# One-core decoder layer: branch and filler weights asked for two slots ahead, negations and DRAM additions of w_down spread over other stages

## The chip, the cores and the metric

One NeuronCore of a Trainium2 chip runs the whole kernel. The metric is the device time of one execution in microseconds. The engines are TensorE (PE, with its weight loads as PEld), VectorE (DVE), ScalarE (ACT), GpSimd (POOL) and SyncE (SP, which here only issues transfers). Each of them works through its own list in order and waits on semaphores.

## The reference

One decoder layer on x (512 tokens, 2048 features, float32), with weights in float32. Cut to what matters here:

```
h = rms_norm(x) ; (q, k, v ..., m_a, m_b) = split(h @ w_in)
y_nsa = nsa_attention(...)          # 8 heads
y_fox = fox_attention(...)          # 8 heads
merged = sigmoid(m_a) * (y_nsa @ w_branch_nsa) + sigmoid(m_b) * (y_fox @ w_branch_fox)
x = x + merged @ w_out
u, v = split(rms_norm(x) @ w_up) ; u = causal_dwconv(u)      # width 3, D_FF = 5632
x = x + (gelu(u) * v) @ w_down
return rms_norm(x)
```

## The kernel before

Products are made to full float32 accuracy from a high and a low part: for weights W, ACT makes `w_hi`, DVE makes `w_lo = w_raw - w_hi`, and PE forms hi·hi, hi·lo and lo·hi. The stages follow each other in time: the paired QKV products (to 580 us), compression of keys and values, NSA (8 heads), merge A (`w_branch_nsa`), FOX (8 heads), merge B (`w_branch_fox`), W_out, the up stage (44 units in a loop), the down stage. QKV, up and down use products of 2x2 blocks in the manner of Strassen; for the down stage sums and differences of blocks of w_down are needed, and they are made ahead of time in DRAM (tensors w_s1, w_s2, w_n3, w_n4, shown as `w_s` and `w_n`).

**Slots.** Outside QKV, up and down, weights come in slots of 1 MB. `w_raw`, `w_hi` and `w_lo` each have two buffers. SP's `load(s, src)` (L493 to L498) waits until `w_lo` of slot s-2 is made, and loads slot s. ACT's `hi(s)` (L1354) waits for the load and for PE to have used slot s-2. DVE's `lo(s)` (L1910) follows it. A merge has 8 slots of 48 matmuls each; slot p makes output blocks 2p and 2p+1.

**Merge.** SP's `load_merge` (L629 on) issues for each slot the weights and, with `load_gates` (L636), the gates of the next slot into one of two buffers `gate_t`. `load_gates(p)` waits until DVE has multiplied the outputs of slot p-2 (semaphore `br_read`). ACT then takes the sigmoid of the gates, and DVE multiplies (L2264; L2266 and L2267 in merge B). ACT's list is sigmoid(p), hi(p+1), sigmoid(p+1), ...; DVE's is lo(p+1), multiply(p), lo(p+2), ...

**Filler.** While a head of NSA or FOX waits for its softmax, PE works on one slot of plain gate blocks (`slot_cols`, L804 to L806). In FOX, SP loads slot S_FOX+2+h at the start of its iteration h (after the store of `o_fox`, L593); ACT makes `hi` of that slot in head h ahead of the head's exponentials (L1555), then POOL scales the probabilities (L2664), and PE transposes them (L1079).

**POOL's background work.** A negation loads a quarter (512 KB) of two w_down blocks into SBUF (L2677), negates it (L2683) and stores it (L2685): 40 of them. A DRAM addition has four steps (L2691 to L2699), with two, two, one and one transfers of 1 MB, of which four accumulate in DRAM: 10 times. Each step waits for the landing of the one before it. Before, negations 0 to 23 stand in QKV, 24 to 31 in merge A and 32 to 39 in merge B; additions 0 and 1 in NSA, 2 and 3 in merge A, 4 and 5 in FOX, 6 and 7 in merge B, 8 and 9 in W_out. In the up stage POOL only multiplies v by the GELU of u (L2746).

**Up stage.** SP loads w_up into `raw` (L697, L700) and stores the product of POOL (L705); a unit takes one turn of about 20 us.

**Start of compression.** SP reads `kv_fm` back (L587, two transfers), loads `sel` (L588), stores the last unit of QKV (L536, L538) and only then goes on. ACT and DVE wait for the landing of that store before `hi` and `lo` of slot S_PRE+1.

## Time and profile before

| | us |
|---|---|
| median of three runs | 2813.95 |
| the runs | 2813.82, 2817.32, 2813.95 |
| the profiled execution | 2819.67 |
| its span | 2817.7 |

The profiled execution is 5.7 us above the median. The stage windows below are in microseconds from the start of its span. PE is busy for 95% of the span, DVE 71%, ACT 43%, POOL 19%.

### The profile page before, as it was taken

How to read it: one execution, taken by the hardware profiler on the slowest of the kernel's cores; microseconds unless marked ns; L12 is line 12 of the kernel's file. 1: busy time of each engine (PE TensorE's matmuls, PEld its weight loads, DVE VectorE, ACT ScalarE, POOL GpSimd, SP SyncE). 2: the span in 40 equal slices, each digit the busy share in tenths (PEclk: the TensorE clock that was granted, in tenths of full speed). 3: DMA queues.
4: the chain of work that ended last, by engine and by line, in shares of the span. 5: the costliest groups of instructions: out<-in, count | busy, mean ns of one | idle time of the engine just before them, and what ended most of it. 6: DMA issues, size and time to landing. Idle time of an engine off the chain costs nothing.

```text
span 2817.7 us, 39923 instructions
## 1 busy us (share of the span) xinstructions
PE 2674.0 (95%) x14729; PEld 2300.1 (82%) x14729; DVE 2003.6 (71%) x2529; ACT 1225.1 (43%) x1614; POOL 539.4 (19%) x385
## 2 busy tenths in 40 slices
PE   8999999989996888778999999999999999999998
PEld 6899999978885676656888999999999998888886
DVE  5898888855551233224228999999999998888886
ACT  6444444434441133212235555555555554444445
POOL 0144444413433322332100000000000000000002
PEclk9999999999998999988999999999999999999999
DMA  7556666585558977689952544444343545666664
GB/s 226 149 174 195 180 189 184 159 244 153 139 136 235 253 174 199 180 236 268 242 183 83 135 116 118 124 111 129 105 131 104 134 107 188 235 224 224 224 209 150
DMA packets 499190, 489.52 MB, mean 174 GB/s; under 512 B 11566, under 2 KB 376832, under 8 KB 498310
## 3 DMA queue, kind: packets, MB, share of 16 engines
q1 hardware_dynamic: 457204, 371.37, 44.2%
q0 software_dynamic: 36080, 106.33, 15.6%
q10 hardware_dynamic: 5826, 10.76, 1.1%
q8 instruction: 50, 0.82, 0.1%
q14 instruction: 30, 0.25, 0.0%
HBM read 425.46 MB, written 127.96 MB: 196 GB/s over the span
## 4 chain that ended last, share of the span: by engine, by line
PE 81%; DMA 9%; DVE 3%; ACT 3%; issue 2%; SPq 1%; POOL 1%; DVEq 0%; ACTq 0%
PE bank L854 22%; PE bank L863 14%; PE bank L1336 13%; PE bank L856 11%; PE bank L804 6%; PE bank L806 6%; PE bank L805 6%; DMA w_raw<-in_w_branch_nsa_dram 3%; DMA w_raw<-in_w_branch_fox_dram 3%; DMA w_raw<-in_w_in_dram 2%; PE bank L1085 2%; ACT w_hi L1354 1%; PE bank L1079 1%; DVE w_lo L1910 1%; POOL l_fox L2664 1%
## 5 line engine op out<-in xcount | busy, mean ns | idle before, releaser
L1910 DVE TENSOR_TENSOR w_lo<-w_raw,w_hi 128x2048 fp32r<-128x2048 f32 x59 | 136.2, 2308 | 349.4 <-ACT w_hi L1354 349.4
L854 PE MATMUL bank<-hl,ring_hi 128*128 128x512 f32 x1032 | 368.4, 398 | 0.5 <-ACT v_sb L1722 0.5
L1336 PE MATMUL bank<-fold_hi,y_slot 128*128 128x512 f32 x1120 | 344.9, 389 | 0.0
L856 PE MATMUL bank<-hl,ring_lo 128*128 128x256 f32 x1032 | 289.8, 281 | 0.0
L1354 ACT ACTIVATE w_hi<-w_raw 128x2048 fp32r<-128x2048 f32 x59 | 112.9, 1913 | 356.4 <-DMA w_raw<-in_w_branch_fox_dram 107.5
L1336 PEld LDWEIGHTS bank<-fold_hi,y_slot 128*128 128x128 f32 x1120 | 210.3, 188 | 43.7
L2746 POOL TENSOR_TENSOR v_sb<-v_sb,conv_t 128x512 f32<-128x512 f32 x44 | 65.3, 1483 | 919.5 <-ACT conv_t L1736 906.1
L1818 ACT ACTIVATE fold_hi<-x_raw 128x1024 fp32r<-128x1024 f32 x140 | 148.5, 1063 | 201.8 <-PE bank L1336 199.7
L854 PEld LDWEIGHTS bank<-hl,ring_hi 128*128 128x128 f32 x1032 | 194.0, 188 | 46.9 <-ACT v_sb L1722 0.7
L1698 ACT ACTIVATE ring_hi<-s_a 128x1024 fp32r<-128x1024 f32 x129 | 136.9, 1062 | 202.7 <-PE bank L856 107.4
L854 PE MATMUL bank<-hl,q_ring_hi 128*128 128x512 f32 x600 | 215.8, 401 | 2.3 <-issue 1.8
L1336 PE MATMUL bank<-fold_lo,y_slot 128*128 128x512 f32 x560 | 217.8, 389 | 0.0
L856 PEld LDWEIGHTS bank<-hl,ring_lo 128*128 128x128 f32 x1032 | 195.1, 189 | 0.0
L2524 DVE TENSOR_TENSOR fold_lo<-x_raw,fold_hi 128x1024 fp32r<-128x1024 f32 x140 | 172.0, 1230 | 24.3 <-ACT fold_hi L1818 24.3
L804 PE MATMUL bank<-y_hi,w_hi 128*128 128x512 f32 x256 | 111.7, 436 | 80.6 <-DVE w_lo L1910 80.6
L804 PE MATMUL bank<-hl,w_hi 128*128 128x512 f32 x448 | 181.9, 406 | 4.4 <-DVE w_lo L1920 3.8
L806 PE MATMUL bank<-hl,w_lo 128*128 128x512 f32 x448 | 176.5, 394 | 0.0
L805 PE MATMUL bank<-hl,w_hi 128*128 128x512 f32 x448 | 176.0, 393 | 0.0
L856 PE MATMUL bank<-hl,q_ring_lo 128*128 128x256 f32 x600 | 169.2, 282 | 0.0
L2345 DVE TENSOR_TENSOR ring_lo<-raw,ring_hi 128x1024 fp32r<-128x1024 f32 x129 | 161.8, 1255 | 5.6 <-ACT ring_hi L1698 2.7
L2345 DVE TENSOR_TENSOR ring_lo<-s_a,ring_hi 128x1024 fp32r<-128x1024 f32 x129 | 157.5, 1221 | 6.0 <-ACT ring_hi L1698 5.9
L1416 ACT ACTIVATE q_ring_hi<-q_sum 128x1024 fp32r<-128x1024 f32 x75 | 79.6, 1061 | 161.5 <-DVE q_sum L2015 95.6
(388 smaller groups left out, 7137.5 us busy)
## 6 DMA issues: line engine op xcount, KB each, us to landing
raw<-in_w_up_dram SPq DMA_DIRECT2D x43, 1024.0 KB, 7.1
raw<-in_w_up_dram SPq DMA_DIRECT2D x86, 512.0 KB, 7.5
w_s<-in_w_down_dram POOLq DMA_DIRECT2D x30, 1024.0 KB, 13.1
x_raw<-in_w_down_dram SPq DMA_DIRECT2D x30, 1024.0 KB, 5.1
w_raw<-in_w_in_dram SPq DMA_DIRECT2D x26, 1024.0 KB, 7.7
raw<-in_w_in_dram SPq DMA_DIRECT2D x25, 1024.0 KB, 8.6
raw<-in_w_in_dram SPq DMA_DIRECT2D x50, 512.0 KB, 7.2
x_raw<-w_s SPq DMA_DIRECT2D x20, 1024.0 KB, 5.5
```

The lines of the kernel that those rows point to most:

```text
L804: mm(dst, l_hi, r_hi, start=first, stop=False)
L805: mm(dst, l_hi, r_lo, start=False, stop=False)
L806: return mm(dst, l_lo, r_hi, start=False, stop=final)
L854: mm(pb[bank][:], hi[:, w], high_low(y[0][:, k, :], y[1][:, k, :]), start=first and k == 0, stop=False, skip_group_check=True)
L856: last = mm(pb[bank][:, 0:TH], lo[:, w], y[0][:, k, :], start=False, stop=k == KH - 1, skip_group_check=True)
L863: last = mm(pb[bank][:, 0:TH], left[:, w], y[z][:, k, :], start=first and k == 0 and n == 0, stop=k == KH - 1 and n == 2, skip_group_check ...
L1336: last = mm(pb[banks[tt]][:], y[:, z, k, tk], right[:, w], start=first and k == 0 and m == 0, stop=k == 3 and m == 2, skip_group_check=True)
L1354: A(w_hi[:, s.par, :], w_raw[:, s.par, :], ACT.Copy).then_inc(w_hi_done, 1)
L1818: A(fold_hi[k % RING][:], x_raw[b][:, 1024 * h:1024 * h + 1024], ACT.Copy).then_inc(piece_hi, 1)
L1910: V.tensor_tensor(w_lo[:, s.par, :], w_raw[:, s.par, :], w_hi[:, s.par, :].bitcast(F32), ALU.subtract).then_inc(w_ready, 1)
L2345: V.tensor_tensor(ring_lo[b][:], src, ring_hi[b][:].bitcast(F32), ALU.subtract).then_inc(piece_ok, 1)
L2524: V.tensor_tensor(fold_lo[b][:], x_raw[FOLD_AT[p, n] % 4][:, 1024 * h:1024 * h + 1024], fold_hi[b][:].bitcast(F32), ALU.subtract).then_inc ...
```

## The change

1. `load_merge`: the weights of slot p+2 are now issued ahead of the gates of slot p+1; before, the weights of slot p+1 were issued behind the gates of slot p+1, whose issue waits for the multiplied outputs of slot p-1. The weights of slot 1 stand ahead of the stage's other waits. In merge A the last two turns load the first two slots of FOX.
2. FOX: iteration h loads slot S_FOX+3+h instead of S_FOX+2+h.
3. POOL: negations 24 to 28 in merge A (without additions), 29 to 34 one in each of the FOX heads 0 to 5 ahead of the addition step, 35 to 39 in merge B. Additions 2 and 3 in FOX, 4 and 5 after the negations of merge B, 6 to 9 in the up stage, one step after each of the multiplications of units 0 to 15. ACT waits for negation 34 before FOX head 6.
4. Compression: the `q_u` and `q_v` stores stand ahead of the second read of `kv_fm`; `sel` is loaded by POOL.
5. The semaphore `o_put` of the stores of plain blocks is split into two by parity; the waits ask for the same stores.

```diff
-QKV_QUARTERS, MERGE_QUARTERS = 24, 32
+QKV_QUARTERS, MERGE_QUARTERS = 24, 35
...
-        for part, (a, b) in enumerate(((0, 4), (4, 12))):
-            sp.dma_start(kv_fm[:, a:b, :], p_dram[kv_at + a:kv_at + b].rearrange("n p t -> p n t")).then_inc(kv_in[part], 16)
-        sp.dma_start(sel[:], c_sel).then_inc(kv_in[1], 16)
+        sp.dma_start(kv_fm[:, 0:4, :], p_dram[kv_at:kv_at + 4].rearrange("n p t -> p n t")).then_inc(kv_in[0], 16)
         store_qkv(QKV_UNITS - 1)
+        sp.dma_start(kv_fm[:, 4:12, :], p_dram[kv_at + 4:kv_at + 12].rearrange("n p t -> p n t")).then_inc(kv_in[1], 16)
...
+            def load_weights(p):
+                if p < 8:
                     load(slot(base + p), wbr[which][:, :, 256 * p:256 * p + 256], n=256)
+                elif which == 0:
+                    load_block(slot(base + p), PLAIN[p + 4])
+
+            load_weights(1)
...
+            load_gates(0)
+            load_weights(2)
+            load_gates(1)
+            store_plain((11, 21)[which], o_cover[:, 0, :])
+            for p in range(1, 8):
+                load_weights(p + 2)
...
                 if p < 7:
                     load_gates(p + 1)
...
+        load_block(slot(S_FOX + 2), PLAIN[14])
         for h in range(HEADS):
-            load_block(slot(S_FOX + 2 + h), PLAIN[14 + h])
+            if h < HEADS - 1:
+                load_block(slot(S_FOX + 3 + h), PLAIN[15 + h])
...
         pool.wait_ge(y_ok, 2)
-        quarters(6, 2)
+        negatives(QKV_QUARTERS, QKV_QUARTERS + 5)
         for h in range(HEADS):
             pool.wait_ge(fr_ready, h + 1)
             scale(l_fox, 4).then_inc(fp_ready, 1)
-            sums_in_dram(4 + h // 4, h % 4)
+            if h < HEADS - 2:
+                negatives(QKV_QUARTERS + 5 + h, QKV_QUARTERS + 6 + h)
+            sums_in_dram(2 + h // 4, h % 4)
         pool.wait_ge(y_ok, 4)
-        quarters(8, 6)
+        negatives(MERGE_QUARTERS, 4 * FOLD_UNITS)
         for k in range(8):
-            sums_in_dram(8 + k // 4, k % 4)
+            sums_in_dram(4 + k // 4, k % 4)
...
-        with pool.Fori(0, UNITS // 4) as i:
-            for r in range(4):
-                a_out_of(r, i)
+        for n in range(UNITS):
+            a_out_of(n % 4, n // 4)
+            if n < 16:
+                sums_in_dram(6 + n // 4, n % 4)
```

The instructions of PE, ACT and DVE keep their order; only SP and POOL are written in another order. At the start of merge A, SP's list before (L593 stores a block, L636 loads gates, L498 loads weights of a slot):

```order
181 L593 DMA p_dram<-o_nsa 128x512 x2
182 L636 DMA gate_t_93<-p_dram 128x2x512
183 L636 DMA gate_t_94<-p_dram 128x2x512
184 L593 DMA p_dram<-o_cover 128x512
185 L498 DMA w_raw<-in_w_branch_nsa_dram 128x8x256
186 L636 DMA gate_t_93<-p_dram 128x2x512
187 L498 DMA w_raw<-in_w_branch_nsa_dram 128x8x256
188 L636 DMA gate_t_94<-p_dram 128x2x512
```

And the same place now:

```order
180 L592 DMA p_dram<-o_nsa 128x512 x2
181 L498 DMA w_raw<-in_w_branch_nsa_dram 128x8x256
182 L635 DMA gate_t_93<-p_dram 128x2x512
183 L498 DMA w_raw<-in_w_branch_nsa_dram 128x8x256
184 L635 DMA gate_t_94<-p_dram 128x2x512
185 L592 DMA p_dram<-o_cover 128x512
186 L498 DMA w_raw<-in_w_branch_nsa_dram 128x8x256
187 L635 DMA gate_t_93<-p_dram 128x2x512
```

Two weight transfers (slots 1 and 2) have moved ahead of the second gates and of the `o_cover` store; from there on each weight transfer belongs to a slot one further on than before. Merge B has the same rows.

In FOX, POOL's list of one head before (`l_fox` is scaled, then an addition step):

```order
239 L2664 TENSOR_SCALAR l_fox<-l_fox,st 128x512
240 L2664 TENSOR_SCALAR l_fox<-l_fox,st 128x384
241 L2664 TENSOR_SCALAR l_fox<-l_fox,st 128x128
242 L2664 TENSOR_SCALAR l_fox<-l_fox,st 128x256
243 L2691 DMA w_n<-in_w_down_dram 512x512
244 L2692 DMA w_s<-in_w_down_dram 512x512
```

And now:

```order
219 L2675 TENSOR_SCALAR l_fox<-l_fox,st 128x512
220 L2675 TENSOR_SCALAR l_fox<-l_fox,st 128x384
221 L2675 TENSOR_SCALAR l_fox<-l_fox,st 128x128
222 L2675 TENSOR_SCALAR l_fox<-l_fox,st 128x256
223 L2688 DMA nb_late<-in_w_down_dram 128x2x512
224 L2694 TENSOR_SCALAR nb_late<-nb_late 128x1024
225 L2696 DMA w_n<-nb_late 128x2x512
226 L2702 DMA w_n<-in_w_down_dram 512x512
227 L2703 DMA w_s<-in_w_down_dram 512x512
```

A whole negation (load, negate, store) has come in between the scaling and the addition step of heads 0 to 5.

## Rows read from the trace of the kernel before

**Rows 1.** Shares of the chain that ended last, by line (the page)

```profile
PE bank L854 22%; PE bank L863 14%; PE bank L1336 13%; PE bank L856 11%; PE bank L804 6%; PE bank L806 6%; PE bank L805 6%; DMA w_raw<-in_w_branch_nsa_dram 3%; DMA w_raw<-in_w_branch_fox_dram 3%; DMA w_raw<-in_w_in_dram 2%; PE bank L1085 2%; ACT w_hi L1354 1%; PE bank L1079 1%; DVE w_lo L1910 1%; POOL l_fox L2664 1%
```

**Rows 2.** Busy time by stage: merge A, FOX, merge B, up; then PEclk, DMA share, GB/s

```profile
844.00:980.20 136.20, 100.23 (x385) 79.63 (x385) 27.75 (x23) 21.91 (x15) 50.06 (x33) 0.89 0.93 246
980.20:1157.00 176.80, 152.25 (x720) 120.25 (x719) 59.98 (x123) 62.69 (x122) 44.61 (x44) 0.94 0.71 178
1174.00:1316.60 142.60, 100.09 (x377) 79.25 (x378) 45.97 (x40) 27.31 (x18) 51.13 (x36) 0.86 0.92 245
1560.00:2360.00 800.00, 800.00 (x5155) 725.09 (x5154) 742.03 (x931) 414.97 (x541) 60.01 (x40) 1.00 0.44 117
```

**Rows 3.** The chain in one slot of merge A: start us, us, what

```profile
901.13 12.03 DMA w_raw<-in_w_branch_nsa_dram
...
913.18 1.92 ACT w_hi L1354
...
917.33 1.29 DVE m L2264 x2
...
918.64 0.36 SPq L636
```

**Rows 4.** Timeline of PE in one slot of merge A: 1st, 10th and 48th matmul

```profile
917.55 0.79 PE L804 MATMUL bank<-y_hi,w_hi 128*128 128x512 f32 x1 [5.19 <-DVE w_lo L1910]
...
921.30 0.40 PE L804 MATMUL bank<-y_hi,w_hi 128*128 128x512 f32 x1
...
929.95 0.39 PE L806 MATMUL bank<-y_hi,w_lo 128*128 128x512 f32 x1
```

**Rows 5.** DMA queues in QKV, NSA and merge A: packets, MB, share of 16 engines

```profile
q0 software_dynamic: 6768, 24.64, 13.0%
...
q0 software_dynamic: 4975, 13.11, 36.7%
...
q0 software_dynamic: 6993, 20.45, 61.3%
q1 hardware_dynamic: 13672, 13.75, 30.9%
```

**Rows 6.** POOL's timeline in merge A: load of a quarter, negation

```profile
859.29 0.74 POOL L2677 DMA_DIRECT2D nb_late<-in_w_down_dram  x1 [9.37 <-DMA w_n<-nb_late]
...
864.20 3.02 POOL L2683 TENSOR_SCALAR nb_late<-nb_late 128x1024 f32<-128x1024 f32 x1 [2.49 <-DMA nb_late<-in_w_down_dram]
```

**Rows 7.** POOL's timeline in FOX: first heads and the last one

```profile
997.03 4.27 POOL L2664 TENSOR_SCALAR l_fox<-l_fox,st 128x512 f32<-128x512 f32 x4 [23.58 <-DVE st L2299]
...
1024.65 4.27 POOL L2664 TENSOR_SCALAR l_fox<-l_fox,st 128x512 f32<-128x512 f32 x4 [21.69 <-DVE st L2299]
...
1041.83 4.26 POOL L2664 TENSOR_SCALAR l_fox<-l_fox,st 128x512 f32<-128x512 f32 x4 [11.26 <-DVE st L2299]
...
1150.81 4.26 POOL L2664 TENSOR_SCALAR l_fox<-l_fox,st 128x512 f32<-128x512 f32 x4 [18.60 <-DVE st L2299]
```

**Rows 8.** Additions in FOX: five of them, and head 0's second alone (us to landing)

```profile
w_s<-in_w_down_dram POOLq DMA_DIRECT2D x5, 1024.0 KB, 11.8
...
w_s<-in_w_down_dram POOLq DMA_DIRECT2D x1, 1024.0 KB, 15.3
```

**Rows 9.** Up stage: a wait of DVE, and timelines of SP and POOL

```profile
DVE s_a L2350 <- DMA raw<-in_w_up_dram: 1.1, 6, 0.3
...
1725.53 0.37 SPq L700 DMA_DIRECT2D raw<-in_w_up_dram  x1
...
1731.68 1.56 POOL L2746 TENSOR_TENSOR v_sb<-v_sb,conv_t 128x512 f32<-128x512 f32 x1 [17.17 <-ACT conv_t L1736]
```

**Rows 10.** The chain at the start of compression: start us, us, what

```profile
590.02 9.67 DMA p_dram<-q_v
...
599.71 1.92 ACT w_hi L1354
...
604.10 6.69 DMA w_raw<-in_w_in_dram
```

More of the change, by code:

```diff
@@ L636, in load_gates @@
                 sp.dma_start(gate_t[p % 2][:], p_dram[a:a + 2].rearrange("n p t -> p n t")).then_inc(g_in[p % 2], 16)
-            for p in range(8):
-                if p:
+            def load_weights(p):
+                if p < 8:
                     load(slot(base + p), wbr[which][:, :, 256 * p:256 * p + 256], n=256)
-                if p == 0:
-                    if which == 0:
-                        sp.wait_ge(qkv_put[1], 16 * QKV_UNITS)
-                        sp.wait_ge(o_put, 16 * (11 + 2))
-                        sp.wait_ge(npv_done, 2 * HEADS + 1)
-                    else:
-                        sp.wait_ge(o_put, 16 * (21 + 2))
-                        sp.wait_ge(fpv_done, HEADS + 1)
-                    load_gates(0)
+                elif which == 0:
+                    load_block(slot(base + p), PLAIN[p + 4])
+            load_weights(1)
+            if which == 0:
+                sp.wait_ge(qkv_put[1], 16 * QKV_UNITS)
+                sp.wait_ge(o_put[0], 16 * 6)
+                sp.wait_ge(o_put[1], 16 * 5)
+                sp.wait_ge(npv_done, 2 * HEADS + 1)
+            else:
+                sp.wait_ge(o_put[0], 16 * 11)
+                sp.wait_ge(o_put[1], 16 * 10)
+                sp.wait_ge(fpv_done, HEADS + 1)
+            load_gates(0)
[4 more added lines that the diff above has]
+                load_weights(p + 2)
                 if p == 6 and which == 1:
-                    sp.wait_ge(o_put, 16 * (22 + 2))
+                    sp.wait_ge(o_put[1], 16 * 11)
                 if p < 7:
                     load_gates(p + 1)
-                if p == 0:
-                    store_plain((11, 21)[which], o_cover[:, 0, :])
         load_merge(S_BA, 0)
@@ L1376, in _ @@
             act.wait_ge(xt_ready, k + 1)
-            A(h_hi[:, k, :], pb[4 + k % 4][:], ACT.Copy, scale=cols[:, G_ATTN + k:G_ATTN + k + 1]).then_inc(xh_done, 1)
+            A(h_hi[:, k, :], pb[4 + k % 4][:], ACT.Copy, scale=cols[:, G_ATTN + k:G_ATTN + k + 1])
             A(m32[:, k, :], pb[4 + k % 4][:], ACT.Copy, scale=cols[:, G_ATTN + k:G_ATTN + k + 1]).then_inc(xm_done, 1)
@@ L2148, in _ @@
         lo(slot(S_PRE + 2))
-        plain_out(0, o_pre[:, 0, :], 0, slot(S_PRE))
+        plain_out(0, 0, o_pre[:, 0, :], 0, slot(S_PRE))
         lo_parts(slot(S_PRE + 3), 3)
@@ L2154, in _ @@
         lo(slot(S_PRE + 5))
-        plain_out(1, o_pre[:, 1, :], 1, slot(S_PRE + 3))
+        plain_out(1, 0, o_pre[:, 1, :], 1, slot(S_PRE + 3))
         lo_parts(slot(S_QN), 4)
@@ L2182, in q_low @@
             V.tensor_tensor(q_lo[:], q_n[:], q_hi[:].bitcast(F32), ALU.subtract).then_inc(ql_ok, 1)
-        plain_out(2, o_pre[:, 0, :], 0, slot(S_QN))
+        plain_out(0, 1, o_pre[:, 0, :], 0, slot(S_QN))
         q_low(0)
@@ L2234, in nsa_step @@
                 V.tensor_copy(pt_n[:, 512:1024], pb[6][:]).then_inc(nt_dve, 1)
-            plain_out(s + 3, o_nsa[:, 1 - g, :], 1 - g, done)
+            plain_out(1 - g, it + (g + 3) // 2, o_nsa[:, 1 - g, :], 1 - g, done)
             if not isinstance(s, int) or s < HEADS - 1:
@@ L2253, in merge @@
             lo(slot(base))
-            plain_out((11, 21)[which], o_cover[:, 0, :], 2, slot(base - 1))
+            plain_out(1, (5, 10)[which], o_cover[:, 0, :], 2, slot(base - 1))
             for p in range(8):
@@ L2289, in _ @@
         lo(slot(S_FOX + 1))
-        plain_out(12, o_fox[:, 0, :], 0, slot(S_FOX))
+        plain_out(0, 6, o_fox[:, 0, :], 0, slot(S_FOX))
         def fox_step(h, b, use, done, fill, more):
@@ L2302, in fox_step @@
             V.tensor_copy(pt_f[:, 512:1024], pb[6][:]).then_inc(ft_dve, 1)
-            plain_out(h + 13, o_fox[:, 1 - b, :], done.par, done)
+            plain_out(1 - b, use + (b + 13) // 2, o_fox[:, 1 - b, :], done.par, done)
             if more:
@@ L2713, in _ @@
                 negative_out((n - 1) // 4, (n - 1) % 4)
+        pool.wait_ge(prod_done, QKV_PRODUCTS)
+        pool.dma_start(sel[:], c_sel).then_inc(wg_loaded, 16)
         for s in range(HEADS):
@@ L2722, in _, with negatives @@
             sums_in_dram(s // 4, s % 4)
-        def quarters(first, sums):
-            for k in range(8):
-                n, q = first + k // 4, k % 4
-                negative_in(n, q)
-                sums_in_dram(sums + k // 4, k % 4)
-                negative_out(n, q)
+        def negatives(first, last):
+            for k in range(first, last):
+                negative_in(k // 4, k % 4)
+                negative_out(k // 4, k % 4)
         pool.wait_ge(y_ok, 2)
-        quarters(6, 2)
+        negatives(QKV_QUARTERS, QKV_QUARTERS + 5)
         for h in range(HEADS):
```

30 lines of the change are left out of this document (16 added, 14 removed).

## The prediction

> **What bounds the kernel now.** I read the chain of work first. Nearly all of it is PE, but three weight transfers stand in it with 8% between them, w_branch_nsa, w_branch_fox and w_in [rows 1]. So PE is the bound except where it waits for weights of the slot stages. The busy times by stage say where: in merge A PE is busy for 100.2 of 136.2 us, in merge B for 100.1 of 142.6, in FOX for 152.3 of 176.8, and in the up stage for all of the 800 us read [rows 2]. The granted clock says the same a second time: 0.89, 0.86 and 0.94 of full speed in those three, 1.00 in the up stage.
>
> Then one slot of merge A in the chain, in order of time. The transfer starts at 901.13 and takes 12.03, `hi` starts at 913.18 and takes 1.92, DVE makes `lo` and begins its two multiplications at 917.33, which take 1.29, SP issues the next gates at 918.64 and only then the next weights [rows 3]. Transfer, `hi`, `lo`, multiplication and issue are one ring of 18 us with PE outside it. PE waits 5.19 us, starts at 917.55, reaches its 10th matmul at 921.30 and its 48th at 929.95 [rows 4]. From the 10th to the 48th that is 8.65/38 = 0.228 us each (the 2.4 GHz level); the nine before took 3.75 where nine of these take 2.05 (mostly the 1.2 GHz level, after the wait). A slot without a wait is 48 x 0.228 = 10.9 us.
>
> **The change, part by part**, against the profiled execution's own 2819.67 us (5.7 above the median, so I take the difference over to 2813.95).
>
> *Merges.* The weights of slot p+2 are asked for as soon as `lo` of slot p is made, about when PE starts slot p. Call E the end of slot p on PE. ACT may then make `hi` of slot p+2 (1.92 us) and DVE `lo` (from 915.10 to 917.33, 2.2 us), ready at E+4.2, and PE needs it at E+10.9. The weights for that have had from the start of slot p to E, and may be late by 6.7 us more: 17.6 us in all, against 12.03 in rows 3. The gates of slot p+1 leave SP 1.4 us after the end of slot p-1 and have some 15 us. In merge B DVE adds two multiplications and at times `hl`, and still fits in 10.9. So PE becomes the bound. Merge A: 136.2 - 8 x 10.9 = 49 us. Merge B: 142.6 - 87.2 = 55 us. Both include the low clock. I take off 1 us for the first slots. **Term: -103.**
>
> Is there bandwidth for it? The DMA shares give engine time per MB, over windows of 520, 185 and 140 us [rows 5]: negations in QKV 0.130 x 520 / 24.64 = 2.7 us, additions in NSA 0.367 x 185 / 13.11 = 5.2 us, SP's transfers in merge A 0.309 x 140 / 13.75 = 3.1 us. Merge A checks the sum: 8.4 MB of negations and 12 MB of additions give 86 us, and 0.613 x 140 is 86. In the new merge A a slot of 10.9 us has 1.57 MB of weights and gates (4.9 us) and about 0.8 of a negation (2.3 us), a share near 0.66 where it was 0.93 [rows 2]. The additions that made merge A dense are gone. POOL's own turn there: load 4.9 us, negation 3.0 [rows 6], store (9.4 us behind the additions, of which little should be left): 13 us, five times 13 is 65 and fits into 87.
>
> *FOX.* `hi` of the next filler stands ahead of the exponentials on ACT, so a late w_in transfer holds up the whole head. POOL's scalings start at 997.03, 1024.65 and 1041.83: one turn of 27.6 and one of 17.2, and seven turns to 1150.81 take 153.8, a mean of 22.0 [rows 7]. Loading a head earlier takes this stall away; seven turns of 17.2 would save 33.
>
> But now POOL's list decides. After the scaling (4.3 us) it has the negation: load 4.9, negate 3.0, store issue 1.1, and then an addition step with 1 to 1.7 us of issue, about 15 us in all, if the load comes at once. Its transfer stands behind the addition step of the previous head on the same queue, which takes 11.8 us to its landing, and 15.3 for the second of two transfers [rows 8]. Stepping through the heads with that order: the first turn is 17, the following four are about 22, 20, 20 and 20, since POOL can't scale before the negation is done. Then ACT waits for the landing of negation 34 before head 6: it is stored some 22 us after the scaling of head 5, lands at 26, and `hi` and the exponentials (4.4) follow, so that turn is about 30. The last is 17. Sum 147, or 7 less than 153.8. If the load did not wait for the additions, five turns stay at 17.2 and the turn before head 6 is 22: sum 125, 29 less. The bound on the other side is a stage no shorter than now, 0. The engines' time per head would be 2.9 + 8.2 + 7 = 18 us, which also speaks for the long end. **Term: -8**, between 0 and -29.
>
> The Trainium skill, "DMA: Bandwidth & Descriptors", section "Queues, rings and completion order", says that an engine takes the descriptors of one ring in their order and goes round between rings. By that rule the negation's load waits behind the additions and the FOX term is -7; without it, -29. That POOL waited 9.37 us for a store issued behind an addition step agrees [rows 6].
>
> *Additions in the up stage.* Here they meet a stage without slack in PE and with DVE busy for 742 of 800 us [rows 2], 1.4 us of idle time in a turn of 19.9. The second half of u is loaded just in time: SP issues it at 1725.53, and DVE waited for it six times, at most 0.3 us [rows 9]. An addition step is issued after POOL's multiplication at 1731.68, so at 1733.3, and lands 11.8 later at 1745.1; the next critical load leaves SP one turn after 1725.53, at 1745.4. The single steps just miss it. The two-transfer step 0 (15 us, four of 16) covers it and may cost DVE 2 to 4 us, against a ring of four pieces of which three products of 2.9 us are in front, and 1.4 us a turn to catch up. **Term: +2**, between 0 and +42 (each step delays the load by 4 us, 1.4 absorbed, 16 times 2.6). W_out keeps eight addition steps, earlier than now: 0.
>
> *Compression.* The store of `q_v` takes 9.67 us behind 3 MB of `kv_fm` [rows 10]. With 1 MB ahead, and at 3.1 us per MB, it lands at about 595; `hi` then starts after the xs parts instead of at 599.71, 4.4 us earlier. The w_in transfer of 604.10 is issued earlier too but has the same bytes ahead of it. **Term: -3**, between 0 and -4.4. `sel` on POOL and the split semaphore: 0, since PE needs `sel` some 30 us after it is issued, and the stores waited for are the same.
>
> Sum: -103 - 8 + 2 - 3 = -112. 2819.67 - 112 = 2707.7 for the profiled execution, and 2813.95 - 112 = **2702** for the median.
>
> **The rivals.**
> (a) *FOX runs free*: the negation is not held up by the additions, 21 us more: 2681. For it: no row shows this order on POOL. Against: rows 6.
> (b) *The up stage is hit*: +42 instead of +2: 2742. For it: DVE's 1.4 us. Against: the timing above, by which 12 of 16 steps miss the load. The same section of the Trainium skill has the rings served in turn, so that a transfer beside additions gets a part of each engine only; by that rule a step that overlaps costs the load up to its own length again, 4 us, and the time is between 2702 and 2742 as the overlap falls.
> (c) *Weights still late in the merges*: if a transfer needs 22 us with two in flight, two slots take 22 + 4.3, a turn is 13.2, 14 turns lose 2.3 each: 32 us, 2734. Against: the share of 0.66.
> (d) *Slower than before*: in the up stage POOL waits for the landing of the last addition step before it issues the next and multiplies; `taps` on ACT and the store on SP wait for POOL. From a landing of 18.1 us on (19.9 less 1.8 of issue) POOL sets the turn; the saving is used up when 16 turns lose 7 us each, at a landing of 25 us: 2815 and above. The longest step seen is 15 to 16 us at a share of 0.9.
> (e) *The change doesn't do what it says*: a wait keeps the second weight transfer back, since `load(s)` needs `lo` of slot s-2. It is made before the turn begins in all four places; then only FOX and the start gain, 11 - 2 = 9: 2805.
>
> **How the numbers follow.** The forecast has 0.58, (a) 0.14, (b) 0.13, (c) 0.08, (e) 0.03, (d) 0.04. The forecast's own range is 2690 to 2716. For 8 in 10 the range takes in (a) and most of (b) and (c): 2678 to 2740. A measurement of this kernel can tell about 0.2%, 5.6 us, from no change. Faster by more than that: all but (d), 0.95; within: 0.01; slower: 0.04.
>
> **What would show it.** In the merges: PE idle near zero and a turn of 10.9 at a granted clock near 1.00, 87 us each. If the turn is above 12, (c), and ACT's `w_hi` waits for a DMA there. In FOX: no w_in transfer in the chain, POOL's scalings 20 us apart in heads 1 to 5 and 30 once; if they are 17 apart, (a). In the up stage: DVE's wait for `raw` above 0.3 us in the first 16 units and PE below 100% there would be (b); POOL never the releaser of ACT, or it is (d). At 590 to 600: `q_v` landing 5 us earlier. The sum is most in danger from FOX's order and from the meeting of additions and loads in the up stage.

## The result and the profile after

| | before | after |
|---|---|---|
| median of four runs | 2815.64 us (2813.82 to 2819.61) | 2693.94 us (2691.52 to 2694.83) |
| profiled execution, span | 2817.7 us | 2693.0 us |
| granted TensorE clock, mean | 0.978 | 0.994 |

The ratio of the means is 0.9565, with a 95% interval of 0.9548 to 0.9581. The forecast was 2702 with a range of 2678 to 2740.

First the stages. This is the table of busy times of the changed kernel: the stretch in us, then its length, PE, PE's weight loads, DVE, ACT and POOL, then the granted clock, the DMA share and GB/s. The rows are merge A, FOX with both its ends, merge B and the up stage; they answer to [rows 2].

```profile
841.80:928.90 87.10, 87.10 (x386) 72.11 (x385) 28.75 (x23) 22.77 (x15) 20.57 (x14) 1.00 0.62 200
928.90:1106.10 177.20, 162.95 (x777) 128.59 (x775) 67.47 (x128) 72.43 (x130) 74.27 (x63) 0.97 0.86 230
1106.10:1193.30 87.20, 87.19 (x385) 72.19 (x386) 43.52 (x40) 27.55 (x18) 24.79 (x18) 1.00 0.81 254
1437.00:2237.00 800.00, 800.00 (x5156) 725.19 (x5155) 745.06 (x932) 415.98 (x542) 82.21 (x62) 1.00 0.60 148
```

In both merges PE is now busy for the whole stretch at full clock. In the up stage it is busy for 800 of 800 us as before, though the DMA share there went from 0.44 to 0.60. What is left is in FOX. The chain of work that ended last can't be set beside [rows 1] as a whole: in this profile it goes back only to 1076.7 us, to the last heads of FOX. In merge B, which it covers, it is PE alone. For what lies before, the waits of PE from 841 to 1200 us say the same; these are all of them (us in all, times, longest):

```profile
PE bank L1086 <- POOL l_fox L2675: 11.6, 3, 7.4
PE bank L810 <- DVE kf_lo L2296: 1.3, 6, 0.2
PE bank L810 <- DVE w_lo L1920: 1.3, 1, 1.3
```

In the kernel before, PE waited 36.0 us in merge A and 44.6 in merge B for `w_lo`. The `w_in` weights of FOX held ACT up once, for 4.4 us, where before they did so five times and for 43.9 us.

To account for the difference I cut both traces at the same events: POOL's last multiplication of QKV, the first and the last matmul on `y` of each merge, POOL's first multiplication of the up stage, the end. The stretches of all runs in this document are cut in this way.

| stretch | before | after | difference | term of the prediction |
|---|---|---|---|---|
| start to the end of QKV | 586.63 | 584.45 | -2.2 | none |
| to merge A (compression, NSA) | 257.19 | 257.36 | +0.2 | -3 |
| merge A | 136.04 | 86.82 | -49.2 | -49 |
| to merge B (FOX and its ends) | 194.12 | 177.48 | -16.6 | -8 |
| merge B | 144.16 | 86.96 | -57.2 | -55 |
| to POOL's first multiplication (W_out) | 236.94 | 236.58 | -0.4 | 0 |
| up and down stage | 1262.62 | 1263.35 | +0.7 | +2 |
| sum | 2817.7 | 2693.0 | -124.7 | -112 (with +1 for first slots) |

The -2.2 at the start is no effect of the change that I can name. The same stretch took between 584.3 and 587.0 us in the profiles of the kernels below, though all of them but e11 have the changed kernel's start.

The merges of the kernel before differ from run to run as well. e11 below is that kernel with one wait that changes nothing: its merges took 139.2 and 135.0 us, together 6 less than in the table, and its span is 6.2 us shorter. So some 6 of the 106.4 us that the merges gained may belong to the run that was profiled, and the medians differ by 121.7 us, not by 124.7.

### The profile page after: what moved, and what is told of

Read it like the earlier page. It is cut to its first block, busy times and chain, and to the rows that moved or that the text cites. A ratio compares the mean times of both kernels' runs of the same rounds, so it can differ in the third digit from the quotient of the medians.

```text
span 2693.0 us, 39815 instructions
## 1 busy us (share of the span) xinstructions
PE 2642.5 (98%) x14729; PEld 2281.9 (85%) x14729; DVE 2004.5 (74%) x2529; ACT 1227.1 (46%) x1614; POOL 533.2 (20%) x386
## 3 DMA queue, kind: packets, MB, share of 16 engines
q0 software_dynamic: 36112, 106.36, 16.5%
## 4 chain that ended last, share of the span: by engine, by line
PE 57%; DMA 1%; ACT 1%; DVE 1%; issue 0%; SPq 0%; DVEq 0%; ACTq 0%
PE bank L860 15%; PE bank L1343 14%; PE bank L869 9%; PE bank L862 7%; PE bank L810 4%; PE bank L812 4%; PE bank L811 4%; DMA d_raw<-in_w_down_dram 1%; PE bank L1224 0%; DMA p_dram<-o_fox 0%; DVE y_lo L2262 0%; ACT sq L1673 0%; ACT m L1682 0%; DVE w_lo L1920 0%; DVE hl L2351 0%
## 5 line engine op out<-in xcount | busy, mean ns | idle before, releaser
L2535 DVE TENSOR_TENSOR fold_lo<-x_raw,fold_hi 128x1024 fp32r<-128x1024 f32 x140 | 172.0, 1230 | 24.4 <-ACT fold_hi L1828 24.4
L2356 DVE TENSOR_TENSOR ring_lo<-raw,ring_hi 128x1024 fp32r<-128x1024 f32 x129 | 167.2, 1297 | 4.0 <-ACT ring_hi L1708 2.5
L1708 ACT ACTIVATE ring_hi<-raw 128x1024 fp32r<-128x1024 f32 x129 | 136.3, 1056 | 24.3 <-PE bank L869 22.9
```

The costliest lines, as they stand in the source:

```text
L1708: A(ring_hi[b][:], src, ACT.Copy).then_inc(piece_hi, 1)
L2356: V.tensor_tensor(ring_lo[b][:], src, ring_hi[b][:].bitcast(F32), ALU.subtract).then_inc(piece_ok, 1)
L2535: V.tensor_tensor(fold_lo[b][:], x_raw[FOLD_AT[p, n] % 4][:, 1024 * h:1024 * h + 1024], fold_hi[b][:].bitcast(F32), ALU.subtract).then_inc ...
```

## Experiments

### What makes the gain in the merges: the order of the loads or POOL's list?

The change does both at once, so each was run alone. Beside the three groups of experiments the kernel before had medians of 2812.57 (e1, e2, e3, e5), 2813.28 (e4, e6, e7, e8) and 2814.26 us (e9 to e12). The split semaphore of the plain stores is in all variants of the changed kernel and was not tested alone.

e1 has the new loads with POOL's old list: eight times load, addition step, negation and store in each merge, addition steps alone in FOX, eight in W_out and none in the up stage:

```diff
-        negatives(QKV_QUARTERS, QKV_QUARTERS + 5)
+        quarters(6, 2)
         for h in range(HEADS):
             ...
-            if h < HEADS - 2:
-                negatives(QKV_QUARTERS + 5 + h, QKV_QUARTERS + 6 + h)
-            sums_in_dram(2 + h // 4, h % 4)
+            sums_in_dram(4 + h // 4, h % 4)
         ...
-        negatives(MERGE_QUARTERS, 4 * FOLD_UNITS)
+        quarters(8, 6)
         for k in range(8):
-            sums_in_dram(4 + k // 4, k % 4)
+            sums_in_dram(8 + k // 4, k % 4)
         ...
-            if n < 16:
-                sums_in_dram(6 + n // 4, n % 4)
```

> The loads are in the order of the changed kernel, POOL's list is that of the kernel before: eight negations and eight addition steps in each merge, addition steps alone in FOX, eight in W_out, none in the up stage. Theory 1, the order of the loads makes the gain: both merges run at 87 us, FOX at its turns without negations, 2685 to 2700. Theory 2, it takes both: in merge A of the kernel before the transfers filled 0.92 of 140 us, 129 us of engine time, and POOL's list ran from 844 to 973.8, 130 us. None of that gets less, so PE may leave merge A early but POOL reaches the first scaling of FOX no earlier than 130 us after the merge began, where the changed kernel has it at 104. Then each merge stretch gives 15 to 25 us at most and the time is 2765 to 2795. I hold theory 2.

e2 has POOL's new list, and in the merges the old order of the loads (the first two slots of FOX are asked for behind merge A again, the rest of FOX's loads stay as changed):

```diff
-            load_weights(1)
             ...
-            load_gates(0)
-            load_weights(2)
-            load_gates(1)
             ...
-            for p in range(1, 8):
-                load_weights(p + 2)
+            for p in range(8):
+                if p:
+                    load(slot(base + p), wbr[which][:, :, 256 * p:256 * p + 256], n=256)
                 ...
                 if p < 7:
                     load_gates(p + 1)
```

> POOL's list is that of the changed kernel; in both merges the weights of slot p+1 are asked for behind the gates again, as in the kernel before (the loads of FOX stay as changed). The ring of a slot was 18 us with a transfer of 12.0, so 6.1 us of it are hi, lo, multiplication and issue. With the thinner traffic of the changed kernel 1 MB lands in about 6.5 us. Theory 1, the ring stays but is shorter: turns of 12.5 to 14 us instead of 10.9, 13 to 25 us more in each merge, time 2715 to 2745. Theory 2, the thinner traffic alone made the gain: same as the changed kernel, 2694. Theory 3, the transfer stays near 12 us because requests queue behind each other: turns of 16 to 18, 2780 or more. I hold theory 1, 2728.

Measured: e1 2744.02 us (2736.17 to 2748.59), e2 2747.74 us (2746.70 to 2749.28). e1's four runs spread over 12 us, and the profiled one, 2736.17, is the shortest, so that its stretches add up to some 8 us less than its median. The stretches:

| | merge A | to first FOX scaling | seven FOX turns | merge B | W_out | time |
|---|---|---|---|---|---|---|
| before | 136.0 | 17.2 | 153.8 | 144.2 | 236.9 | 2815.6 |
| e1, new loads, old POOL | 89.9 | 42.0 | 120.8 | 92.8 | 260.3 | 2744.0 |
| e2, old loads, new POOL | 97.5 | 17.2 | 137.5 | 130.6 | 236.6 | 2747.7 |
| after | 86.8 | 17.2 | 137.2 | 87.0 | 236.6 | 2693.9 |

In e1 the merges themselves are nearly as short as in the changed kernel. But POOL's list has not become shorter, and it comes due in the stage behind. This is POOL's timeline of e1 at the end of that list (start, duration, engine and line, operation, and in brackets the idle time before it with its releaser):

```profile
968.94 2.76 POOL L2694 TENSOR_SCALAR nb_late<-nb_late 128x1024 f32<-128x1024 f32 x1 [4.70 <-DMA nb_late<-in_w_down_dram]
971.99 0.81 POOL L2696 DMA_DIRECT2D w_n<-nb_late  x1 [0.30 <-POOL nb_late L2694]
972.84 4.27 POOL L2675 TENSOR_SCALAR l_fox<-l_fox,st 128x512 f32<-128x512 f32 x4
```

The first scaling of FOX starts the moment the last store is issued, with no idle time in brackets: POOL was late. PE waited for it, and behind merge B ACT waited for the last negation of the second list. From the waits between 930 and 980 us of PE, and between 1205 and 1260 us of ACT (us in all, times, longest), first PE:

```profile
PE bank L1086 <- POOL l_fox L2675: 17.9, 1, 17.9
```

and of ACT:

```profile
ACT w_hi L1361 <- DMA w_n<-nb_late: 34.1, 1, 34.1
```

So the place and the mechanism of my theory 2 were right (I had put the first scaling 130 us after the start of merge A, it came after 132), but its total, 2765 to 2795, was at least 20 us too long, because I left the turns of FOX as they were. They fell to 17.3, which is the subject of the next section.

In e2 the ring of a slot is still there, with a shorter transfer in it. These are pieces of the chain in merge B of e2; the columns are start, duration, and what the chain went through:

```profile
1131.82 6.92 DMA w_raw<-in_w_branch_fox_dram
1138.76 1.92 ACT w_hi L1357
...
1144.96 1.12 DVE m L2274
1146.57 6.75 DMA w_raw<-in_w_branch_fox_dram
...
1178.73 14.45 DMA w_raw<-in_w_branch_fox_dram
```

With negations beside them alone the two transfers shown first take 6.8 to 6.9 us where [rows 3] had 12.0, and a turn is 14.7. The transfer of 14.45 us starts 0.4 us before POOL issues the first addition step of W_out's list, and from it to the next request are 24.4 us. In merge A, where no additions are, the turns of e2 are 12.2 to 12.7. So thinning POOL's traffic alone saves 38.5 us in merge A and only 13.5 in merge B (4.4 against e11's merge B). Here the forecast missed: I had 13 to 25 us more than the changed kernel in each merge and 2728 in all. It was 10.7 in merge A and 43.6 in merge B, because I had not counted that W_out's list of additions begins in merge B, behind the last negation. The new order alone saves 46 and 51, and gives 48 back behind the merges. By the ratios to the kernel before measured beside them (0.9752 and 0.9759, each within 0.005, against 0.9565), e1 has about 57% of the gain and e2 about 55%. They are not two halves that add up: both have the new loads of FOX.

### FOX: what held up the turns before, and what holds them up now?

The prediction had two statements here: the late `w_in` transfer makes the long turns of [rows 7], and in the changed kernel POOL's negation takes its place. Four kernels take these apart. e5 puts the filler weights one head later again, as before; the negations stay:

```diff
-        load_block(slot(S_FOX + 2), PLAIN[14])
         for h in range(HEADS):
-            if h < HEADS - 1:
-                load_block(slot(S_FOX + 3 + h), PLAIN[15 + h])
+            load_block(slot(S_FOX + 2 + h), PLAIN[14 + h])
```

> The changed kernel with the filler weights of FOX asked for one head later again, as in the kernel before. Theory 1, late w_in weights made the long turns of the kernel before (27.6, 24.1, 27.6, 23.8 us): they come back, FOX at 153 instead of 137 from first to last scaling, and more with negations between, 2708 to 2715. Theory 2, POOL's list sets turns of 17 to 21 us anyway and covers the late weights: 0 to 3 us more, 2694 to 2697. I hold something between, nearer to theory 1: 2705.

e3 takes the negations out of FOX:

```diff
-QKV_QUARTERS, MERGE_QUARTERS = 24, 35
+QKV_QUARTERS, MERGE_QUARTERS = 24, 32
...
-        negatives(QKV_QUARTERS, QKV_QUARTERS + 5)
+        negatives(QKV_QUARTERS, MERGE_QUARTERS)
...
-            if h < HEADS - 2:
-                negatives(QKV_QUARTERS + 5 + h, QKV_QUARTERS + 6 + h)
```

> The changed kernel with the six negations of FOX taken out: eight stand in merge A and eight in merge B, the addition steps stay where they are. Theory 1, POOL's list with the negation in it sets the turns of FOX: without it seven turns of 17.2 us, 120.5 instead of the 137.2 of the changed kernel, 16 us less, 2677, if POOL's three more negations in merge A (12.2 us each, the fifth stored at 898.5) end by 936, before the first scaling at 945.8. Theory 2, the traffic in FOX (share 0.88) sets the turns: the share falls to 0.77, turns stay above 18, less than 8 us gained, 2686 or more. The turn of 27 us before head 6, where ACT waits for the landing of the last negation, goes in both: 9.7 us of the 16.

e4 moves only the last of them, from head 5 to merge A (`+ 6` for `+ 5`, and `HEADS - 3` for `HEADS - 2`):

> The changed kernel with the last negation of FOX taken out of head 5: six negations in merge A, one in each of heads 0 to 4. It tests what makes the turn of 27.0 us before head 6. Theory 1, ACT waits there for the landing of the last negation, stored some 17 us after the scaling of head 5: with head 4 as the last it has landed a turn earlier, the turn becomes 17 to 18, FOX's seven turns 128 instead of 137, time 2684 to 2686. Theory 2, it is the traffic at that place (a first addition step of two transfers and a weight transfer): the turn stays at 22 to 27, time 2690 to 2694.

e8 leaves the negations and takes the addition steps out:

```diff
-            sums_in_dram(2 + h // 4, h % 4)
...
         for k in range(8):
-            sums_in_dram(4 + k // 4, k % 4)
+            sums_in_dram(2 + k // 4, k % 4)
...
-            if n < 16:
-                sums_in_dram(6 + n // 4, n % 4)
+            if n < 24:
+                sums_in_dram(4 + n // 4, n % 4)
```

> The changed kernel with no addition step in FOX: the negations stay there, W_out keeps eight steps and the up stage gets 24 turns with one instead of 16. Two questions. In FOX: if the negation's load waited 6.6 to 10.2 us because it stood behind the additions on POOL's queue, it now waits 3.5 to 4.5, the turns are 17.3 and the one before head 6, where ACT waits for the landing of the last negation, 18 to 20: 122 to 125 instead of 137. If the wait comes from the other traffic of FOX it stays above 6 and the turns at 18 to 20. In the up stage: my rival (b) priced a step that collides with a load at 2.6 us; by it 8 more steps cost up to 21 us; by the trace of the changed kernel (PE without a wait there) they cost 0, and the stretch from the first multiplication of POOL to the end stays at 1263.4. With both as I expect, 2680 to 2683.

| | the seven turns from scaling to scaling | sum | time |
|---|---|---|---|
| before | 27.6, 17.2, 24.1, 17.0, 27.5, 16.5, 23.8 | 153.8 | 2815.6 |
| e5, old loads, negations | 20.1, 20.4, 18.5, 19.9, 17.1, 26.5, 17.0 | 139.5 | 2698.50 (2697.63 to 2699.06) |
| after: new loads, negations | 17.4, 18.4, 20.8, 19.6, 17.4, 27.0, 16.5 | 137.2 | 2693.94 |
| e4, the last one out | 17.4, 22.0, 19.3, 17.4, 16.9, 15.8, 17.5 | 126.3 | 2690.70 (2684.00 to 2694.36) |
| e8, negations, no additions | 17.4, 17.4, 17.4, 17.4, 17.3, 21.9, 14.8 | 123.7 | 2679.47 (2679.11 to 2679.93) |
| e3, additions, no negations | 16.3, 17.5, 17.3, 17.4, 17.3, 17.3, 17.3 | 120.5 | 2680.00 (2678.73 to 2680.70) |

*The negation behind the additions.* This is POOL's timeline over head 1 in the changed kernel:

```profile
963.21 4.28 POOL L2675 TENSOR_SCALAR l_fox<-l_fox,st 128x512 f32<-128x512 f32 x4 [3.27 <-DVE st L2310]
967.44 0.78 POOL L2688 DMA_DIRECT2D nb_late<-in_w_down_dram  x1
976.56 2.77 POOL L2694 TENSOR_SCALAR nb_late<-nb_late 128x1024 f32<-128x1024 f32 x1 [8.34 <-DMA nb_late<-in_w_down_dram]
979.63 0.78 POOL L2696 DMA_DIRECT2D w_n<-nb_late  x1 [0.30 <-POOL nb_late L2694]
980.41 0.53 POOL L2705 DMA_DIRECT2D w_s<-w_n  x1
980.93 1.16 POOL L2706 DMA_DIRECT2D w_s<-in_w_down_dram  x1
981.66 3.82 POOL L2675 TENSOR_SCALAR l_fox<-l_fox,st 128x512 f32<-128x512 f32 x3
```

And the same place in e8:

```profile
967.30 0.76 POOL L2688 DMA_DIRECT2D nb_late<-in_w_down_dram  x1
971.55 2.76 POOL L2694 TENSOR_SCALAR nb_late<-nb_late 128x1024 f32<-128x1024 f32 x1 [3.48 <-DMA nb_late<-in_w_down_dram]
974.61 0.78 POOL L2696 DMA_DIRECT2D w_n<-nb_late  x1 [0.30 <-POOL nb_late L2694]
980.51 4.28 POOL L2675 TENSOR_SCALAR l_fox<-l_fox,st 128x512 f32<-128x512 f32 x4 [5.12 <-DVE st L2310]
```

The load of the same 512 KB holds POOL for 8.34 us with an addition step ahead of it on its queue, and for 3.48 without one. Over heads 1 to 5 this wait is 6.56 to 10.22 against 3.39 to 3.52; in head 0, where the queue is empty, the changed kernel has 3.52 too. So it is the additions, not the rest of FOX's traffic, which e8 has as well. In the first fence POOL is late for the scaling at 981.66 (no idle time before it); in the second it waits 5.12 us for DVE. The Trainium skill, "DMA: Bandwidth & Descriptors", section "Queues, rings and completion order", has each engine consume a ring's descriptors in their order (it says so of the queues of SP and ACT); the wait on POOL's queue agrees. No run here put the additions on another queue, which would separate order from mere company.

*The turn of 27.* In the waits of ACT between 929 and 1106 us, the changed kernel has one long wait for the last negation's store (us in all, times, longest):

```profile
ACT w_hi L1361 <- DMA w_n<-nb_late: 11.3, 1, 11.3
```

It is gone in e4, and the turn is 15.8 where it was 27.0. But e4's four runs spread over 10 us where those of e3, e5 and e8 spread over 1 to 2, and reach into those of the changed kernel (2691.52 to 2694.83). The profiled one is the shortest, 2684.00, and the median is 2690.70; already in the profiled one the turn of head 1 is 22.0, where the changed kernel has 18.4. What the longer runs did isn't in a profile, and stays open.

*What had held up the kernel before.* With neither the old loads nor negations in the way (e3, and e1 from its first scaling on) the turn is 17.3, and PE no longer waits for POOL's scaling at all: that is PE's own time. The old order of the loads costs 33 us without negations (before against e3 or e1), but only 2.4 with them (e5 against after). I had not expected that; my number for e5 was 2705, and it gave 2698.50. The 2.4 is no more than the turns vary by themselves: in e6 and e12 below, which have the changed kernel's FOX, they sum to 134.4 and 137.1. In the kernel before the addition step of head 0 was issued straight behind the scaling, and the `w_in` weights 4 us later. In head 1 it was the other way round. POOL's timeline of the kernel before:

```profile
1001.26 1.05 POOL L2691 DMA_DIRECT2D w_n<-in_w_down_dram  x1
1001.98 0.98 POOL L2692 DMA_DIRECT2D w_s<-in_w_down_dram  x1
...
1028.88 0.55 POOL L2694 DMA_DIRECT2D w_s<-w_n  x1
1029.43 1.15 POOL L2695 DMA_DIRECT2D w_s<-in_w_down_dram  x1
```

And SP's:

```profile
1005.36 0.42 SPq L498 DMA_DIRECT2D w_raw<-in_w_in_dram  x1
...
1022.42 0.38 SPq L498 DMA_DIRECT2D w_raw<-in_w_in_dram  x1
```

The chain of the kernel before gives the transfer asked for at 1005.36, 4.1 us behind the additions, 14.77 us. The one of 1022.42 is asked for 6.5 us ahead of them, and `hi` at 1037.40 had no wait for it. The turns are 27.6 and 17.2. In e5 the negation stands between scaling and additions, so these leave POOL 12.3 us after the scaling of head 0 instead of 4.2, later still in heads 1 to 5, and in each of heads 0 to 5 behind the `w_in` request. A piece of e5's chain shows what it takes then:

```profile
971.88 9.29 DMA w_raw<-in_w_in_dram
```

So the negation that delays POOL in FOX also takes the additions out of the way of the weights. The stall is smaller, not gone: ACT waits for `w_in` in e5 six times, 24.9 us in all and 5.4 at most, where in the kernel before it was 43.9 us and 11.9 at most. In heads 1 to 4 of e5 POOL waits 2.0 to 6.0 us for DVE before it scales, so there the weights set the turns of 18.5 to 20.4, where in the changed kernel POOL's list sets turns of about the same length. That is the other reason why the two sums lie so close. The part on the additions rests on the order of the rows in two kernels; no run had the old loads in FOX with the additions taken out. The run that was to show it alone failed to make the edit count: in the kernel before, POOL was to issue a head's addition step only when the bias of the next head has landed.

```diff
             scale(l_fox, 4).then_inc(fp_ready, 1)
+            if h < HEADS - 1:
+                pool.wait_ge(bf_loaded[(h + 1) % 2], (h + 1) // 2 * 16 + 16)
             sums_in_dram(4 + h // 4, h % 4)
```

> The kernel before with one edit: in FOX POOL issues the addition step of a head when the bias of the next head has landed, which SP asks for right behind the w_in weights, where it issued it straight behind the scaling. Loads stay in their old order, no negation is in FOX. Theory 1: FOX's long turns (27.6, 24.1, 27.6, 23.8) came from the addition step that starts 4 us ahead of the w_in transfer and lengthens it to 11 to 15 us; the change moved it behind the w_in transfer by putting the negation first, and that alone mends most of it. Then the turns become 17 to 19 here, the seven turns 120 to 130 instead of 153.8, and the time falls by 24 to 33 us, to 2781 to 2790. Theory 2: only an earlier request for w_in mends it, because the additions of one head or the other always overlap: turns stay as they are or shift, 2805 to 2815.

It gave 2813.41 us (nine runs from 2810.94 to 2835.14, a tenth of 10014.02), a ratio of 1.0001 (0.9979 to 1.0023), with turns of 27.7, 16.9, 23.8, 16.6, 27.5, 16.6 and 24.6. The reason stands in its POOL timeline:

```profile
998.99 4.26 POOL L2664 TENSOR_SCALAR l_fox<-l_fox,st 128x512 f32<-128x512 f32 x4 [25.60 <-DVE st L2299]
1003.21 1.05 POOL L2691 DMA_DIRECT2D w_n<-in_w_down_dram  x1
```

The addition step still follows the scaling at once. The bias of head 1 is asked for right behind that of head 0, long before the scaling; the wait should have been on the bias of head h + 2. The run decides nothing between its theories.

### The compression

e6 puts both parts of `kv_fm` and `sel` ahead of the last stores of QKV again, and takes `sel` off POOL's list:

```diff
-        store_qkv(QKV_UNITS - 1)
         sp.dma_start(kv_fm[:, 4:12, :], p_dram[kv_at + 4:kv_at + 12].rearrange("n p t -> p n t")).then_inc(kv_in[1], 16)
+        sp.dma_start(sel[:], c_sel).then_inc(kv_in[1], 16)
+        store_qkv(QKV_UNITS - 1)
```

> The changed kernel with the compression's transfers in the order of the kernel before: both parts of kv_fm and sel ahead of the last stores of QKV. Theory 1, my term: the last store of q_v lands 4 to 5 us later and the stretch from QKV to merge A gets 3 us longer (257.4 becomes 260), time 2697. Theory 2, the gain of the first hi was lost at the next one, since the weights behind kv_fm land no earlier: the stretch stays at 257, time 2694, the same within 1 us.

It gave 2694.23 us (2693.70 to 2695.24) and a stretch of 257.2: nothing. Where the gain went is seen on ACT. The changed kernel:

```profile
592.77 1.90 ACT L1361 ACTIVATE w_hi<-w_raw 128x2048 fp32r<-128x2048 f32 x1
601.03 1.91 ACT L1361 ACTIVATE w_hi<-w_raw 128x2048 fp32r<-128x2048 f32 x1 [6.37 <-DMA w_raw<-in_cmp_w_k_dram]
605.59 2.19 ACT L1370 ACTIVATE w_hi<-w_raw 128x512 fp32r<-128x512 f32 x4 [2.64 <-DMA w_raw<-in_w_in_dram]
```

`hi` no longer waits for the store of `q_v` and starts at 592.77; the kernel before had it at 599.71 [rows 10], in a run that was 2.2 us later there. That is 4.7 us of gain, as forecast. But the next weights land at 601.0, as the kernel before had them at 603.1: they stand behind 2 MB of `kv_fm` in both orders. e7 moves these 2 MB behind the next two weight transfers:

```diff
         store_qkv(QKV_UNITS - 1)
-        sp.dma_start(kv_fm[:, 4:12, :], p_dram[kv_at + 4:kv_at + 12].rearrange("n p t -> p n t")).then_inc(kv_in[1], 16)
         ...
         load_w1(slot(S_PRE + 2), 0, 1)
         load_block(slot(S_PRE + 3), PLAIN[1])
+        sp.dma_start(kv_fm[:, 4:12, :], p_dram[kv_at + 4:kv_at + 12].rearrange("n p t -> p n t")).then_inc(kv_in[1], 16)
```

> The changed kernel with the second part of kv_fm (2 MB, used 30 us later) behind the next two weight transfers of the compression. If these 2 MB are what holds up the second compression weights (issued at 586.71, hi at 601.03) and the w_in block (hi at 605.59), both come 4 to 8 us earlier, of the 8.8 us that PE waits there 3 to 6 go, the stretch from QKV to merge A becomes 252 to 254 instead of 257.4, time 2689. If the wait only moves once more (to the weights of the v side, which then stand behind the 2 MB), 257 and 2694.

ACT's timeline at the same place in e7:

```profile
594.65 1.90 ACT L1361 ACTIVATE w_hi<-w_raw 128x2048 fp32r<-128x2048 f32 x1
597.32 1.91 ACT L1361 ACTIVATE w_hi<-w_raw 128x2048 fp32r<-128x2048 f32 x1 [0.78 <-DMA w_raw<-in_cmp_w_k_dram]
605.75 2.20 ACT L1370 ACTIVATE w_hi<-w_raw 128x512 fp32r<-128x512 f32 x4 [6.52 <-DMA w_raw<-in_w_in_dram]
```

The second `hi` now comes 2.7 us behind the first instead of 8.3. The stretch is 253.3 instead of 257.4, and in it PE waits 5.3 us for `w_lo` instead of 8.8. The median is 2690.34 us (2689.55 to 2694.43), 3.9 less than e6 measured beside it. The profiled run is the longest of the four: it began with a stretch 1.9 us longer than in the changed kernel's profile, and its merge B is 1.6 us longer, where PE waits 2.5 us for `w_lo` instead of 1.3. So not all that is gained here need reach the end.

### The up stage

e8 has answered for 24 single steps: the up and down stages took 1262.8 us with them, against 1263.4 with 16 and 1262.6 with none. e9 puts the 16 steps into eight turns:

```diff
-            if n < 16:
-                sums_in_dram(6 + n // 4, n % 4)
+            if n < 8:
+                for k in (2 * n, 2 * n + 1):
+                    sums_in_dram(6 + k // 4, k % 4)
```

> The changed kernel with the 16 addition steps of the up stage in eight turns, two a turn, where they stood one a turn. The second step is issued when the first has landed, 12 to 15 us later, and the next multiplication of POOL comes behind that. Rival (d) is the mechanism: POOL's turn is then two landings and 1.6 us, 26 to 30 us, where the stage's turn is 19.9. After eight turns POOL is 50 to 60 us late; SP holds the weights behind the store of two units before, which gives one to two turns of slack (20 to 40 us): up stage 15 to 40 us longer, 2710 to 2735, and SP or ACT waits for POOL. Rival (b), shares of the engines: 16 steps at 2.6 us, up to 42 more, DVE waiting for raw. If neither bites, 2694 and POOL late but nobody waiting.

It gave 2730.11 us (2729.23 to 2731.64), and 1298.1 us for the two stages, 34.7 more. POOL over one turn:

```profile
1505.27 1.66 POOL L2760 TENSOR_TENSOR v_sb<-v_sb,conv_t 128x512 f32<-128x512 f32 x1
1516.53 1.05 POOL L2708 DMA_DIRECT2D w_s<-in_w_down_dram  x1 [9.60 <-DMA w_s<-in_w_down_dram]
1529.04 1.01 POOL L2710 DMA_DIRECT2D w_n<-w_s  x1 [11.46 <-DMA w_s<-in_w_down_dram]
1529.68 1.67 POOL L2760 TENSOR_TENSOR v_sb<-v_sb,conv_t 128x512 f32<-128x512 f32 x1
```

A turn is two landings and the multiplication: 24 to 26 us, once 32.6, where the stage needs 19.9. ACT waits for it directly, and DVE waits for its weights. From the waits of ACT between 1424 and 1800 us (the changed kernel has none for POOL):

```profile
ACT conv_t L1742 <- POOL v_sb L2760: 51.9, 6, 11.5
```

And of DVE in the same stretch, where the changed kernel has 5.9 us and at most 2.0 between 1437 and 1760 us:

```profile
DVE s_a L2361 <- DMA raw<-in_w_up_dram: 20.4, 10, 6.6
```

Rival (d)'s mechanism is real. It needs two landings a turn. Whether the engines' share (rival b) adds to the 34.7 can't be told from this run, since both waits are there.

### Both savings together

e10 is e3 with e7's order. It ran beside the changed kernel on one chip (e12 is the changed kernel once more).

> No negation in FOX (eight in each merge) and the second part of kv_fm behind two weight transfers, together. They lie in different stretches, so the gains add: 13.9 and 3.6 us from medians, 14 and 4 from the stretches (FOX 137 to 120.5, QKV to merge A 257.4 to 253.3). 2676 if they add. If the earlier merge A or the traffic in merge B takes one of them back (PE waited 2.5 us there with the late kv_fm alone), 2679.

> The changed kernel once more, beside the others on one chip: 2694, within 2 us. The stretches as in its first profile: merges 87 each, seven turns of FOX 134 to 138, 257 from QKV to merge A, 1263 from POOL's first multiplication to the end.

Measured: e10 2676.51 us (2674.71 to 2677.90), e12 2695.25 us (2694.11 to 2700.36). No run of the one lies within the runs of the other. The ratio of the medians is 0.9930; against the kernel before e10 has 0.9502 (0.9475 to 0.9528). Its turns of FOX sum to 119.9, its stretch to merge A is 254.7. It is the fastest version measured.

## Why the prediction was right, step by step

- **Merges, -103: right, and for the reason given.** Measured are -49.2 and -57.2, of which some 6 us may be the profiled run of the kernel before (e11). PE at 87 us each is 8 x 10.9 as the 48 matmuls gave. Merge B was 2 us short because my window ended at 1316.6, with merge B running to 1318.4. The share of 0.66 was measured as 0.62. It was not the condition that I took it for: e1 has a share of 1.01 in merge A, and PE is at 87.6 of 90.1 us. e1 and e2 add what the prediction used but did not stress: it counted thinner traffic only as a condition, while POOL's shorter list itself is worth about as much, because the work would otherwise have come due in FOX and W_out. By the old list e1 loses 24.8 and 23.8 us there.
- **FOX, -8: right in kind, too small by 9 us.** The turns were forecast as 17, 22, 20, 20, 20, 30 and 17 (their sum is 146, which gives the -8, and not 147), and came as 17.4, 18.4, 20.8, 19.6, 17.4, 27.0 and 16.5. The term that was mis-sized is POOL's list. I took 4.9 us for a load from merge A of the kernel before [rows 6]; on a queue with nothing ahead of it it is 3.5, so that head 0's additions leave POOL 12.3 us after the scaling. For the load behind them I counted 15.3 us to their landing and the load's own 4.9 behind it, 20 us from their issue at 958.12; it had landed by 976.5, after 18.4. The one was 1.4 us too much, the other 1.6, and that is most of the second turn's 18.4 instead of 22. The turn of head 4 was 17.4 and not 20, since the load there landed after a wait of 6.56 us. The turn before head 6 was 27 because the store was issued 18.5 us after the scaling, not 22.
- **What the FOX term said of the loads: wrong in its weight.** "Loading a head earlier takes this stall away" holds (e1: 120.8). But with the negation between scaling and additions most of the stall is gone without it (ACT waits 24.9 us for `w_in` in e5 and 43.9 before), and what is left hides behind POOL's list; the new order of the loads is then worth 2.4 us of the turns, and 4.6 of the medians.
- **Compression, -3: wrong, 0.** The step that failed is "`hi` then starts after the xs parts, 4.4 us earlier". It did start earlier, and nothing came of it, since the next weights stood behind the same 2 MB. I looked at the `w_in` transfer behind it and not at the `w_cmp` weights between. e7 shows that these 2 MB were the cause.
- **Up stage, +2: 0 within what can be read (+0.7).** DVE's longest wait for `raw` was 2.0 us, within the 2 to 4 forecast, and the ring of pieces absorbed it. Rival (b) is out at this density and also with 24 steps.
- **Rivals.** (a) did not occur: the negation's load was held up behind the additions, as the reason against it has it. e8, where nothing holds it up, is what it would have been: 123.7 us for the seven turns and 2679.5 in all, where (a) had 125 and 2681. (c) did not occur: PE's only wait in a merge is 1.3 us for `lo` at the entry of merge B. (e) did not occur: both merges take 87 us. (d) did not occur at one step a turn; it is a mechanism that e9 brings out with two landings in a turn.

## What to carry to other kernels

When requests are moved ahead and background work is thinned in one change, run each half alone: here the one gave about 57% of the gain and the other 55%, and the first handed part of what it won to the next stage, where a list that had not shrunk came due. Look for a transfer that a later step waits for and that is issued behind a long one of the same engine: here the wait for a 512 KB load was 6.6 to 10.2 us in that place and 3.4 to 3.5 without the additions, and either list moved out of the stage gave 14 us. Moving only the last negation out shortened its turn from 27.0 to 15.8, but the medians differ by 3.2 us only, within the spread of e4's runs. Before pricing an earlier landing, look at the next transfer that the same consumer needs: if it stands behind the same bytes, the gain is lost.

## What the runs showed of the hardware

- In merge A of e1 the DMA engines were busy for the whole 90 us (share 1.01, 290 GB/s), and PE still worked for 87.6 of 90.1 us. With two slots asked for ahead, full engines did not starve it, where the kernel before had PE at 100.2 of 136.2 at a share of 0.93.
- With the loads in the old order, a negation that made the additions of head 0 leave POOL 12.3 us after the scaling instead of 4.2, and those of later heads later still, came with turns of FOX that were 14.3 us shorter in sum (153.8 to 139.5), though it lengthens POOL's own list.
- 24 addition steps beside the up stage cost PE nothing as long as one was issued per turn of 19.9 us; two per turn cost 34.7 us in eight turns.
